# Three pairs of FFN blocks where there were two, and the vector engine's sums in other places of its queue

## What is computed

```python
def _layer(x, c, positions, ...):
    mod = silu(c) @ w_ada + b_ada                 # 6 vectors of 1024
    ...
    h = _rmsnorm(x, g_pre_ffn) * (1.0 + sc2) + sh2
    f = (silu(h @ w_gate) * (h @ w_up)) @ w_down  # 1024 -> 2816 -> 1024
    return x + gt2 * _rmsnorm(f, g_post_ffn)
```

## Time and profile before

| | |
|---|---|
| profiled execution | 851.03 us, of which the span is 849.2 us |
| PE busy | 833.2 us, 98% of the span |
| DVE busy | 686.9 us, 81% |
| ACT busy | 458.9 us, 54% |
| POOL busy | 122.2 us, 14% |
| mean granted clock of PE | 0.995 of full speed |
| moved by DMA | 194.09 MB, mean 229 GB/s |

### The profile page before, as it was taken

How to read it: one execution, slowest core, us unless ns; L and a number is a source line. 1 busy time by engine, 2 the same in 40 slices (tenths; PEclk the granted TensorE clock), 3 DMA queues, 4 the chain that set the end, 5 groups by cost and what they waited for, 6 DMA issues and landing times.

```text
span 849.2 us, 11576 instructions
## 1 busy us (share of the span) xinstructions
PE 833.2 (98%) x4131; PEld 690.4 (81%) x4131; DVE 686.9 (81%) x1180; ACT 458.9 (54%) x732; POOL 122.2 (14%) x92
## 2 busy tenths in 40 slices
PE   8999999999999999999999999999999989999997
PEld 6877888888888888888898788888888777787885
DVE  5898889888788767785789899898778889998753
ACT  5665555555666434433565655556575645555522
POOL 5400400302120030120420040040030000000040
PEclk9999999999999999999999999999999989999999
DMA  8996676575418888787519657666532733807821
GB/s 346 403 369 223 229 257 256 194 276 200 150 51 310 298 289 317 256 327 265 184 74 364 236 198 266 226 245 235 205 131 100 286 136 120 328 27 296 339 80 50
DMA packets 34795, 194.09 MB, mean 229 GB/s; under 512 B 4273, under 2 KB 4529, under 8 KB 17714
## 3 DMA queue, kind: packets, MB, share of 16 engines
q1 hardware_dynamic: 33410, 189.64, 60.2%
q0 software_dynamic: 1328, 3.71, 1.4%
HBM read 192.29 MB, written 1.05 MB: 228 GB/s over the span
## 4 chain that ended last, share of the span: by engine, by line
PE 87%; DVE 5%; DMA 4%; issue 2%; ACT 2%; SPq 0%; DVEq 0%; ACTq 0%
PE ps L1719 23%; PE ps L1721 23%; PE ps L1720 23%; PE ps L1832 4%; DMA wide_t<-scale_first 3%; PE ps L2138 3%; PE ps L1896 2%; DVE w_lo L1156 2%; ACT w_hi L769 1%; DMA raw<-w_stream 1%; PE ps L1757 1%; PE ps L1756 1%; PE ps L1763 1%; PE ps L1917 1%; PE ps L1918 1%
## 5 line engine op out<-in xcount | busy, mean ns | idle before, releaser
L1156 DVE TENSOR_TENSOR w_lo<-raw,w_hi 128x2048 fp32r<-128x2048 f32 (+2 forms) x126 | 286.6, 2280 | 58.9 <-ACT w_hi L769 57.7
L1719 PE MATMUL ps<-w_hi,t_hi 128*128 128x512 f32 (+2 forms) x712 | 282.0, 396 | 1.8 <-DVE w_lo L1156 1.0
L1721 PE MATMUL ps<-w_hi,t_lo 128*128 128x512 f32 (+2 forms) x712 | 275.1, 386 | 0.0
L1720 PE MATMUL ps<-w_lo,t_hi 128*128 128x512 f32 (+2 forms) x712 | 274.5, 386 | 0.0
L769 ACT ACTIVATE w_hi<-raw 128x2048 fp32r<-128x2048 f32 (+2 forms) x128 | 240.6, 1883 | 35.5 <-DMA raw<-w_stream 28.9
L666 POOL PARTITION_ALL_REDUCE wide_t<-wide_t x20 | 81.0, 4052 | 581.7 <-DVE wide_t L1268 580.8
L1719 PEld LDWEIGHTS ps<-w_hi,t_hi 128*128 128x128 f32 x712 | 133.8, 188 | 30.5 <-DVE w_lo L1156 3.0
L1721 PEld LDWEIGHTS ps<-w_hi,t_lo 128*128 128x128 f32 x712 | 133.7, 188 | 27.7
L1720 PEld LDWEIGHTS ps<-w_lo,t_hi 128*128 128x128 f32 x712 | 134.0, 188 | 25.1
L1268 DVE SCALAR_TENSOR_TENSOR wide_t<-ada,cs,wide_t 128x1024 f32<-128x1024 f32 x80 | 110.2, 1377 | 1.2 <-DMA ada<-w_ada 0.7
L1719 PE MATMUL ps<-w_hi,m_hi 128*128 128x512 f32 x208 | 85.3, 410 | 0.0
(11 more groups left out here) (256 smaller groups left out, 1072.5 us busy)
## 6 DMA issues: line engine op xcount, KB each, us to landing
raw<-w_stream SPq DMA_DIRECT2D x124, 1024.0 KB, 5.1
ada<-w_ada SPq DMA_DIRECT2D x80, 512.0 KB, 5.6
wide_t<-gains POOLq DMA_DIRECT2D x7, 512.0 KB, 4.9
mixed<-w_stream SPq DMA_DIRECT2D x3, 1024.0 KB, 8.9
raw<-w_stream SPq DMA_DIRECT2D x4, 656.0 KB, 7.0
mixed<-scale_first SPq DMA_DIRECT2D x2, 1024.0 KB, 10.3
wide_t<-shift_first SPq DMA_DIRECT2D x4, 512.0 KB, 11.0
wide_t<-scale_first SPq DMA_DIRECT2D x2, 1024.0 KB, 12.6
```

The costliest lines, as they stand in the source:

```text
L1156: nc.vector.tensor_tensor(w_lo[:, U % RING, a:n], src[:, a:n], w_hi[:, U % RING, a:n].bitcast(F32), ALU.subtract).then_inc(s_lo, 1)
L1719: nc.tensor.matmul(dst, hi, w_h, start=first, stop=False)
L1720: nc.tensor.matmul(dst, hi, w_l, start=False, stop=False)
L1721: return nc.tensor.matmul(dst, lo, w_h, start=False, stop=last)
```

## The change

`TWINS` becomes `((7,), (5, 8))`: layer 0 pairs blocks 7 and 8, layer 1 pairs 5, 6 and 8, 9 in place of 3, 4 and 6, 7. The counts of pieces change in both layers. The additions change place: the tokens' sums stand three blocks ahead of the first pair, between the gate products of the two tiles; their low part stands so one block later; the first weight addition stays behind the split of e0; the second and third stand between the gate products of the block ahead of a pair. A pair can now hold pieces too.

```diff
-TWINS = ((), (3, 6))
+TWINS = ((7,), (5, 8))
...
     if l + 1 < DEPTH:
-        return (0, 2, 3, 3, 3, 3, 3, 3, 2, 2, 0), (4, 8)
-    return (1, 1, 1, 0, 0, 1, 0, 0, 4, 0, 0), (9,)
+        return (1, 4, 4, 4, 2, 2, 0, 3, 0, 4, 0), (4, 7)
+    return (1, 3, 1, 1, 1, 0, 0, 1, 0, 0, 0), (8,)
...
-            return TWINS[l][0] - 2 if TWINS[l] else N_FF
+            return TWINS[l][0] - 3 if TWINS[l] else N_FF
...
-                if name[0] == "twin" and name[2] in (0, 1, 3):
-                    add_weights(U, name[2])
-
-            def add_weights(U, e):
...
+                if name[0] == "twin" and name[2] == 0:
+                    add_first(U)
+                elif name[0] == "twin" and name[2] == 3:
+                    add_corner(U - 3)
+
+            def add_first(U):
+
+                upper, landed, count = stored(*SOURCE[U + 4])
                 dve.wait_ge(s_lo, U + 1)
...
+                dve.wait_ge(landed, count)
+                nc.vector.tensor_tensor(w_sum, w_sum, upper, ALU.add).then_inc(s_w_sum, 1)
+
+            def add_lower(U):
+
+                upper = stored(*SOURCE[U + 4])[0]
+                lower, landed, count = stored(*SOURCE[U + 5])
+                dve.wait_ge(landed, count)
+                nc.vector.tensor_tensor(upper, upper, lower, ALU.add).then_inc(s_w_sum, 1)
+                dve.wait_ge(s_lo, U + 2)
+                nc.vector.tensor_tensor(w_sum, w_sum, lower, ALU.add).then_inc(s_w_sum, 1)
...
+                many = ffn_pieces(l)[0][j]
+                add_pieces(max(many - 2, 0))
                 split_lo(l, behind[6])
+                add_pieces(min(many, 1))
                 split_lo(l, behind[7])
+                add_pieces(many > 1)
...
-                    if j == sums_step(l):
-                        add_tokens(l)
-                    elif j == sums_step(l) + 1:
-                        sums_low(l)
                     for u in ahead[:1]:
                         split_lo(l, u)
                     add_pieces(max(many - 2, 0))
...
                         gate_m(l, j, t, ps[:, QKT + t, 256:512])
+                        if t == 0 and j == sums_step(l):
+                            add_tokens(l)
+                        elif t == 0 and j == sums_step(l) + 1:
+                            sums_low(l)
+                        elif t == 0 and j + 1 in TWINS[l]:
+                            add_lower(BASE[l] + twin_unit(l, j + 1))
```

More of the change, by code:

```diff
@@ L1157, in split_lo, with add_corner @@
                                         w_hi[:, U % RING, a:n].bitcast(F32), ALU.subtract).then_inc(s_lo, 1)
-                if name[0] == "twin" and name[2] in (0, 1, 3):
-                    add_weights(U, name[2])
-            def add_weights(U, e):
-                start = U - e
-                upper, lower, corner = (stored(*SOURCE[start + i]) for i in (4, 5, 2))
-                dve.wait_ge(s_lo, U + 1)
[L1166 to L1172, removed]
+                if name[0] == "twin" and name[2] == 0:
[4 more added lines that the diff above has]
+                upper, landed, count = stored(*SOURCE[U + 4])
+                dve.wait_ge(s_lo, U + 1)
+                dve.wait_ge(landed, count)
[7 more added lines that the diff above has]
+                nc.vector.tensor_tensor(w_sum, w_sum, lower, ALU.add).then_inc(s_w_sum, 1)
+            def add_corner(U):
+                dve.wait_ge(s_lo, U + 4)
+                nc.vector.tensor_tensor(w_sum, w_sum, stored(*SOURCE[U + 2])[0], ALU.add).then_inc(s_w_sum, 1)
             def add_tokens(l):
```

## The result

The changed kernel took 861.35 us (median of 4 runs, 860.09 to 862.90), the kernel before, run beside it, 852.11 us (851.09 to 852.98): the ratio is 1.0112 with a 95% interval of 1.0093 to 1.0131. It is 9.2 us slower. The profiled execution took 862.90 us, its span is 861.1 us.

A forecast was written before the change was run, and what follows sets the result against it. PE, 87% of the chain, was taken to bound the kernel, with its waits all for DVE. From 851.0 us, -2.7 (third pair) - 10.6 (old waits) + 8.3 + 12.7 (new waits) gave 858.7; forecast 858.5, range 845 to 864.

The forecast's parts named there:

- layer 1, new waits: Layer 1: late additions, splits and loads make PE wait at block 4 and in both pairs, together +8.3 us.
- pair 5, 6: Layer 1's first pair: the unit behind e4's split is again loaded late, 0.8 + 0.4 us.
- pair 8, 9: Layer 1's last pair: reduction delays e4's split to 11 us; e5, e6 wait 3.0 + 1.2, restarts included, plus 1.2 clock chance.
- layer 0, new waits: Layer 0, where PE never waited: waits in blocks 1, 3, 4, 6 and small ones, together +12.7 us.
- block 3: Layer 0: the reduction behind the eighth piece takes 3.7 us of DVE, gate product late by 0.5 + 0.3 us.
- block 4, its clock: Layer 0: late unit loads delay tile 1's gate product, 2.5 + 0.3 us, range 0 to 5; no clock fall counted.
- block 6, its clock: Layer 0: reduction behind the sixteenth piece makes tile 1's gate product 4.3 us late, restart 0.4, clock fall 2.5: 7.2.
- Rival 1: Faster: DVE keeps up, POOL takes nothing from it beside the reductions; blocks 3, 4 met; 843.6 us, 27%.
- part 4: Layer 0's new waits from pieces, sums, late loads and reductions ahead of its pair: +12.7 us.
- Part 3: Layer 1's new waits with the new pairs and places of additions: +8.3 us.
- Part 1: The third pair, in layer 0: 12 matmuls less, -2.7 us; DVE's 30.6 just fits PE's 30.9.
- Rival 2: No help in layer 0: DVE bounds pair 7, 8 and block 9, backlog there and block 10; 861 to 864 us, 11%.

The follow-up runs named there:

- e3: Changed kernel with POOL's reduction behind layer 0's sixteenth piece replaced by a memset (work left out); 855.97 us.
- e2: e1 with layer 1's eighth piece moved into the last pair and its table made in block 10; 844.02 us.
- e1: Changed kernel with layer 0 as before (no pair, old counts of pieces and tables), layer 1 as changed; 848.23 us.
- e5: Changed kernel with the token sums and weight additions at their places of before; 857.97 us.
- e6: Changed kernel with POOL's reduction behind layer 0's eighth piece replaced by a memset (work left out); 858.70 us.
- e7: Changed kernel with layer 0's pieces in threes, five in its pair, and the second table behind block 9; 856.96 us.
- e9: Changed kernel with the next weight unit's load issued ahead of each block's first pieces, in both layers; 858.10 us.
- e10: e8 plus the third pair, the unit's load ahead of the pieces, layer 0's first six blocks taking 1, 4, 4, 4, 3, 1 pieces; 845.98 us.
- e12: As e10, but with 2, 3, 3, 4, 4, 1 pieces in layer 0's first six blocks; 846.46 us.
- e8: e2 with the additions at their old places; 842.05 us.
- e11: e8 plus the third pair, old order of loads, 2, 3, 3, 3, 3, 3 pieces in layer 0's first six blocks; 846.38 us.

## Why the prediction held

The forecast was 858.5 us with a range of 845 to 864, and slower; it measured 861.35. Its own steps, against the trace. The profiled execution took 862.90, so there the sum of 858.7 is 4.2 low. That the forecast missed the median by less, 2.9, is in part luck: that execution is the slowest of the four, and layer 1's 1.1 under its term made up for some of layer 0's 5.5 over.

| term | forecast | measured in the profile |
|---|---|---|
| layer 1, new waits | +8.3 | +7.2 |
| block 4 | 0.6 + 0.3 | 0.58 |
| pair 5, 6 | 0.8 + 0.4 | 0.67 |
| pair 8, 9 | 3.0 + 1.2 | 2.69 + 0.75 |
| layer 0, new waits | +12.7 | +18.2 |
| block 1 | 1.3 | 1.34 |
| block 2 | 0 | 0.35 |
| block 3 | 0.5 | 1.92 |
| block 4, its clock | 2.5, 0 | 3.19, 2.9 |
| block 6, its clock | 4.3, 2.5 | 4.22, 3.0 |

**Rival 1, faster, and part 4, block 6.** It was to be decided by whether POOL takes time from DVE. It does: two instructions took 3.97 and 4.22 us for 2.28 and 2.29 in e3, 3.6 us held over a reduction of 7.47, against 1.7 + 2.0 in the sum. The rest of the walk through block 6 (start 351.48) holds to 0.1 us: e1's split ended at 13.0 and the gate product of tile 1 at 18.1, as forecast. The rule of the Trainium skill (SBUF - State Buffer, section Who interferes with whom) that the sum was weighed against was pieced together from the page: it tells of a lock for the whole instruction where it treats DVE's two-port modes, and of a DVE instruction with two SBUF inputs it says that it contends with a GpSimd instruction that reads SBUF. A hold for the whole of each half doesn't fit: half a reduction lasts some 3.7 us and held DVE 1.7 and 1.9. That DVE with two SBUF inputs and GpSimd reading SBUF hold each other up at all, the trace agrees with.

**Part 3, layer 1.** Right within 1.1 us, the place and the mechanism too (e4's split ended 10.8 us into the last pair, 11 forecast; e2: 4.2 us for the reduction and its piece). The way was partly another: PE waited for product additions that stand behind three splits, rather than for a late load. The chance given to the clock there came out against the fall in this execution; in e1, e5, e6, e7 and e9 the same wait was followed by 0.68 to 0.74.

**Part 4, block 4: the step that failed.** "Counted through" I had block 4 2.5 late from the first reduction and the late loads together, and gave it no fall of the clock, since I held 3.75 us, the one wait with a fall in the trace before, for what is needed. The fall came at 3.19 us and cost 2.9. e6 showed that the reduction has no part in this wait (3.17 without it), e9 that the held piece's load ahead of the unit's makes 1.9 us of it. The size was named as the least sure (0 to 5). Wait and clock together are 3.3 us more than the term of 2.8, the largest part of what the forecast was low.

**Block 3** was mis-sized, 1.92 for 0.5. Without the reduction it is 0.44. I had counted 3.7 us of DVE for it; its rows in the changed kernel are 2.72 and 3.26 us for 2.29 and 1.28, only 2.4 held, as the split began 1.7 us after the reduction. So here the price was too high, and the slack around it counted much too large.

**Part 1** holds nearly: -2.7 forecast; 2.3 seen behind block 6 in e10 and e12. **Rival 2** (the pair and block 9 bound by DVE) did not come in the changed kernel, but 30.6 of 30.9 left nothing: with five pieces in the pair and a reduction beside them it did, in e7.

**Still open.** Whether some spread of the pieces gives the third pair without a wait was not shown: the seven kernels with it that leave nothing out had layer 0 at 165.7 to 178.2 us, against 162.7 without. Nor was e8 tried with the pairs of layer 1 at other blocks.

## To carry to other kernels

Before PE is spared work by sums made on another engine, add up that engine's busy time over the stretch ahead of the place, not its average over the kernel: 2.7 us saved for 27 us of DVE was no bargain once DVE was 95% full, though 81% over the whole span looked like room. In a queue that is worked off in order, put no load that others need behind one that waits for a buffer; here it made 1.9 of a wait of 3.2 us and a fall of the clock, and the engine that seemed to be at fault had been idle for 4.7 us. But what is put ahead in the queue delays what comes behind: block 1 then waited 0.5 us more and got a fall itself. And keep GpSimd's reductions away from the vector engine's full blocks: moving one of them, with its piece, from the block ahead of a pair into the pair gained 4.2 us, more than the third pair could have.

## What was unexpected of the hardware

The fall of TensorE's clock to near 1.2 GHz is not fixed by the length of the wait ahead of it. Waits of 3.17 to 4.30 us were all followed by a fall. Over the next 6 us or so the mean was 0.52 or 0.53 (3.19 and 4.22 in the changed kernel, 4.23 in e6, 3.75 before), 0.65 (4.30 in e9) or only 0.71 to 0.74 (3.52, 3.32, 3.36, 3.34 and 3.17 in e7, e3, e11, e5 and e6): the time at the lower level differed, so that one fall cost between 1.5 and 3.0 us. The same wait of 2.69 us was followed by 1.00 in the changed kernel and in e3, and by 0.68 in e5. Two windows behind the wait in block 1 of layer 0, of e10 (wait 2.06) and of e12 (1.98), in a fence each:

```profile
272.84:278.00 5.16, 5.16 (x17) 4.07 (x18) 4.34 (x5) 2.50 (x3) 0.00 (x0) 0.67 1.03 406
```

```profile
272.48:278.00 5.52, 5.52 (x26) 4.54 (x27) 4.34 (x5) 2.63 (x3) 0.00 (x0) 1.00 1.02 423
```

Nearly the same wait, and a fall worth 5.16 x 0.33 = 1.7 us behind one of them; in e9 1.81 was followed by 0.69, in the changed kernel 1.92 by 1.00. What decides between them no run here shows. Waits up to 1.57 us never were followed by a fall where I looked. The spread of the times is in line with this, no more: the runs of e8, whose only wait is 0.43, lie within 0.33 us, those of e6 within 4.3 and of the changed kernel within 2.8 (of e1 and e3, though, within 1.1).
